# Two reorderings in a one-core two-block transformer kernel: the second long convolution's products and the second attention's value products

## The reference

```python
q_x, k_x, v_x, hy_x = jnp.split(hx @ p["w_in"], cuts, axis=-1)      # 512 tokens
v_c = heads_v(hc @ w_v)                                             # 256 context tokens
v_all = jnp.concatenate([v_c, heads_v(v_x)], axis=2)
attn_x = diff_out(diff_attn_blocked(q_x, k_all, v_all, lam), p["subln"], lam_init)
...
def hyena_mixer(proj, p, k_f):
    u = short_conv(proj, p["hy_conv_w"], p["hy_conv_b"])
    v, x1, x2 = jnp.split(u, HY_ORDER + 1, axis=-1)
    z = v
    for n, gate in enumerate((x1, x2)):
        z = gate * (long_conv(z, k_f[:, n]) + p["hy_skip"][n] * z)
    return rmsnorm(z, p["hy_norm"])
```

## Time and profile before

| | |
|---|---|
| median of three runs | 1535.79 us (1535.58 to 1537.45) |
| the profiled execution's own time | 1538.33 us |
| its span | 1536.5 us |
| PE busy | 1483.9 us, 97% of the span |
| DVE busy | 864.3 us, 56% |
| ACT busy | 621.0 us, 40% |
| POOL busy | 309.2 us, 20% |
| mean granted TensorE clock | 0.986 of full speed |

### The profile page before, as it was taken

How to read it: one execution, slowest core, us unless ns; L and a number is a source line. 1 busy time by engine, 2 the same in 40 slices (tenths; PEclk the granted TensorE clock), 3 DMA queues, 4 the chain that set the end, 5 groups by cost and what they waited for, 6 DMA issues and landing times.

```text
span 1536.5 us, 18015 instructions
## 1 busy us (share of the span) xinstructions
PE 1483.9 (97%) x7022; PEld 1209.0 (79%) x7022; DVE 864.3 (56%) x1398; ACT 621.0 (40%) x986; POOL 309.2 (20%) x296
## 2 busy tenths in 40 slices
PE   6999999999999999999998999999898999999998
PEld 5776768888878878888876878877687888888886
DVE  5455667554577564664457437777656555345434
ACT  5635773232444231334344326664335333123332
POOL 0263211101032100121004312225621111111101
PEclk9999999999999999999998999999999999999999
DMA  7352105655255344554326221223532323322321
GB/s 246 122 163 71 42 28 177 222 162 169 78 184 173 123 165 145 171 161 168 124 96 216 76 69 42 65 100 124 170 118 96 96 96 96 109 87 92 107 86 55
DMA packets 53327, 187.93 MB, mean 122 GB/s; under 512 B 5943, under 2 KB 6616, under 8 KB 53114
## 3 DMA queue, kind: packets, MB, share of 16 engines
q1 hardware_dynamic: 47450, 165.80, 32.8%
q0 software_dynamic: 4736, 16.78, 3.3%
q10 hardware_dynamic: 1056, 4.19, 0.8%
HBM read 174.16 MB, written 12.58 MB: 122 GB/s over the span
## 4 chain that ended last, share of the span: by engine, by line
PE 89%; DVE 4%; ACT 3%; issue 1%; POOL 1%; DMA 0%; SPq 0%; ACTq 0%; DVEq 0%; POOLq 0%
PE PS L458 87%; PE PS L469 2%; DVE wl L1689 1%; ACT wh L1108 1%; DVE TMP L2189 0%; ACT TMP L1201 0%; DMA X<-in_x 0%; DVE TMP L1742 0%; ACT TMP L1199 0%; POOL wl L2329 0%; DVE accm L1669 0%; DVE TMP L2152 0%; ACT TMP L1398 0%; ACT TMP L1212 0%; DVE Y L1704 0%
## 5 line engine op out<-in xcount | busy, mean ns | idle before, releaser
L1689 DVE TENSOR_TENSOR wl<-raw,wh 128x1024 fp32r<-128x1024 f32 x212 | 274.5, 1298 | 282.3 <-ACT wh L1108 281.8
L458 PE MATMUL PS<-HTh,wh 128*128 128x512 f32 x1056 | 420.8, 398 | 8.1 <-ACT TMP L1398 3.9
L458 PE MATMUL PS<-HTl,wh 128*128 128x512 f32 x1056 | 414.2, 392 | 0.0
L458 PE MATMUL PS<-HTh,wl 128*128 128x512 f32 x1056 | 413.9, 392 | 0.0
L1108 ACT ACTIVATE wh<-raw 128x1024 fp32r<-128x1024 f32 x228 | 239.0, 1053 | 280.7 <-PE PS L458 242.3
L458 PEld LDWEIGHTS PS<-HTh,wh 128*128 128x128 f32 x1056 | 200.3, 190 | 56.1 <-issue 12.4
L458 PEld LDWEIGHTS PS<-HTh,wl 128*128 128x128 f32 x1056 | 200.0, 189 | 43.2
L458 PEld LDWEIGHTS PS<-HTl,wh 128*128 128x128 f32 x1056 | 200.4, 190 | 39.0 <-issue 0.5
L458 PE MATMUL PS<-wh,FFh 128*128 128x512 f32 x432 | 169.8, 393 | 0.0
L458 PE MATMUL PS<-wh,FFl 128*128 128x512 f32 x432 | 168.8, 391 | 0.0
L458 PE MATMUL PS<-wl,FFh 128*128 128x512 f32 x432 | 168.8, 391 | 0.0
(11 more groups left out here) (322 smaller groups left out, 2134.7 us busy)
## 6 DMA issues: line engine op xcount, KB each, us to landing
raw<-in_ws SPq DMA_DIRECT2D x268, 512.0 KB, 3.8
taps<-TMP SPq DMA_DIRECT2D x16, 256.0 KB, 2.5
tab<-in_spec POOLq DMA_DIRECT2D x8, 512.0 KB, 5.8
raw<-taps SPq DMA_DIRECT2D x8, 512.0 KB, 3.9
kd<-TMP POOLq DMA_DIRECT2D x16, 256.0 KB, 6.4
wh<-in_wd POOLq DMA_DIRECT2D x8, 512.0 KB, 4.0
wl<-in_wd POOLq DMA_DIRECT2D x8, 512.0 KB, 4.7
kf<-kd SPq DMA_DIRECT2D x8, 512.0 KB, 3.7
```

Source lines behind the costliest of these rows:

```text
L458: return nc.tensor.matmul(out, l, r, start=start, stop=stop, skip_group_check=True)
L1689: tt(WL[k][:, :n], RAW[RAW_AT["unit", u, 0] % RAWS][:, :n], f32(WH[k][:, :n]), ALU.subtract).then_inc(sem("lo_dve"), 1)
```

## The change

- **Values tile by tile.** All six tiles are summed side by side for k = 0 to 5 only. The last two slices are done tile by tile, in the order `V2_TURN` = 1, 2, 3, 4, 0, 5, and `p_v2` is incremented after each. The copies wait for their own tile and go in that order.
- **Second convolution (o = 1).** TensorE issues forward 0 to 3 first, then backward 0 and 1, group 11, turn 10, backward 2 and 3, turn 11. The units of the transform matrices are packed to match (forward 0 to 3 in two units, backward 0 and 1 in one). On VectorE, ScalarE and GpSimd head 3's scaling and short convolution 10 come after spectral 5 and no longer after spectral 4.
- **Banks.** The scaling sum 3 and turn 9 take banks of `ACC`, so `RING4` serves the forward products alone. Each accumulator is asked for when its first product comes, by a fixed table `ACC_TURN`, and no longer all four at once; this holds for o = 0 too.
- **GpSimd.** `sub_low(3 * o)` comes after the low parts of f = 1, for both orders.

No product, copy or transfer is added or removed.

```diff
--- before.py
+++ after.py
@@ -100,4 +100,8 @@
         inv = [[("dft_i", t * 512 + f * P, k * P, P) for t in range(2) for k in range(2)] for f in range(4)]
-        pack(fwd[0] + fwd[1] + fwd[2] + inv[0], "pre")
-        pack(fwd[3] + inv[1], "pre")
+        if o == 0:
+            pack(fwd[0] + fwd[1] + fwd[2] + inv[0], "pre")
+            pack(fwd[3] + inv[1], "pre")
+        else:
+            pack(fwd[0] + fwd[1] + fwd[2] + fwd[3], "pre")
+            pack(inv[0] + inv[1], "pre")
         pack(colmajor("w_in_2", 1536 + (8 if o == 0 else 11) * P, 1))
@@ -397,2 +401,9 @@
 
+        V2_TURN = (1, 2, 3, 4, 0, 5)
+
+        def V2_READY(i):
+
+            return "v2_evv" if i % 2 else "v2_ev", 1 + sum(1 for j in V2_TURN[:V2_TURN.index(i)] if j % 2 == i % 2)
+
+
         EARLY_FIRST = range(2)
@@ -884,9 +895,16 @@
                     spread(3)
-            bs = [bank(("v2", i), "v2_evv" if i % 2 else "v2_ev", i // 2 + 1) for i in range(6)]
-            for k in KT:
+            bs = [bank(("v2", i), *V2_READY(i)) for i in range(6)]
+            def value_step(k, i, w):
+                h, l, o = (HCh, HCl, i) if i < 2 else (HTh, HTl, i - 2)
+                return mm3(PS[:, bs[i], :], (h[:, k, o * P:(o + 1) * P], l[:, k, o * P:(o + 1) * P]), w, k == 0, k == 7)
+
+            for k in range(6):
                 w = weights("w_in_2", k * P, D)
                 for i in range(6):
-                    h, l, o = (HCh, HCl, i) if i < 2 else (HTh, HTl, i - 2)
-                    m = mm3(PS[:, bs[i], :], (h[:, k, o * P:(o + 1) * P], l[:, k, o * P:(o + 1) * P]), w, k == 0, k == 7)
-            m.then_inc(sem("p_v2"), 1)
+                    value_step(k, i, w)
+
+            for i in V2_TURN:
+                for k in (6, 7):
+                    m = value_step(k, i, weights("w_in_2", k * P, D))
+                m.then_inc(sem("p_v2"), 1)
 
@@ -952,2 +970,4 @@
 
+            ACC_TURN = ((6, 7, 4, 5), (7, 5, 4, 6))
+
             def hyena_group(j):
@@ -959,3 +979,3 @@
             def hyena_turn(j):
-                b = bank(("ht", j), "u_ev", j + 1, RING4)
+                b = bank(("ht", j), "u_ev", j + 1, ACC if j == 9 else RING4)
                 e.wait_ge("hc_v", 6 * j + 6)
@@ -974,3 +994,3 @@
             def sub_scale(h):
-                b = bank(("sn", h), "sn_v", h + 1, RING4 if h % 2 else ACC)
+                b = bank(("sn", h), "sn_v", h + 1, RING4 if h == 1 else ACC)
                 e.wait_ge("sn_dg", 4 * h + 4)
@@ -1009,5 +1029,2 @@
                 y = n % 3
-                if f == 0:
-                    for q in range(4):
-                        bank(("acc", o, q), *(("ac_q", 2 * o + q - 1) if q > 1 else ("ac_v", 4 * o + 2 * q + 2)), ACC)
                 for c in range(2):
@@ -1015,2 +1032,6 @@
                     for q in range(2):
+                        if f == 0:
+                            a = 2 * c + q
+                            bank(("acc", o, a), *(("ac_q", 2 * o + a - 1) if a > 1 else ("ac_v", 4 * o + 2 * a + 2)),
+                                 (ACC_TURN[o][a],))
                         i = mm3(PS[:, BANK["acc", o, 2 * c + q], :], weights("dft_i", 512 * c + f * P, q * P, o),
@@ -1028,8 +1049,13 @@
                         sub_scale(1)
-                    if f in (1, 2) and o:
-                        hyena_turn(8 + f)
-                    if f >= 2:
+                    if f == 1 and o:
+                        hyena_turn(9)
+                    if f >= 2 and o == 0:
                         backward(o, f - 2)
+                if o:
+                    backward(o, 0)
+                    backward(o, 1)
 
                 hyena_group(8 + 3 * o)
+                if o:
+                    hyena_turn(10)
                 backward(o, 2)
@@ -1450,4 +1476,6 @@
                     rotated(7)
-            for i in range(0, 6, 2):
-                e.wait_ge("p_v2", 1)
+            for i in V2_TURN:
+                if i % 2:
+                    continue
+                e.wait_ge("p_v2", V2_TURN.index(i) + 1)
                 act(V2[:, i, :], PS[:, BANK["v2", i], :], ACT.Copy, scale=2.0 ** -10).then_inc(sem("v2_ev"), 1)
@@ -1556,3 +1584,3 @@
                         sub_diag(0)
-                    if f == 1 - o:
+                    if f == 1:
                         sub_high(3 * o)
@@ -2084,4 +2114,6 @@
                     rotated(7)
-            for i in range(1, 6, 2):
-                e.wait_ge("p_v2", 1)
+            for i in V2_TURN:
+                if i % 2 == 0:
+                    continue
+                e.wait_ge("p_v2", V2_TURN.index(i) + 1)
                 ts(V2[:, i, :], PS[:, BANK["v2", i], :], 2.0 ** -10, None, ALU.mult).then_inc(sem("v2_evv"), 1)
@@ -2220,5 +2252,5 @@
                         spectral(4 * o + f)
-                    if f == 1 - o:
+                    if f == 1:
                         sub_high(3 * o)
-                    if f == 0 and o:
+                    if f == 1 and o:
                         hyena_conv(10)
```

## The result

The changed kernel takes **1527.19 us** (median of 4 runs, 1526.66 to 1530.0) against 1536.62 for the kernel before (median of 4, 1535.58 to 1537.74): a ratio of 0.9948 [0.9936, 0.9959]. In a later group, with 5 runs of it and 21 of the kernel before, it is 1527.8 against 1535.36, ratio 0.9954 [0.9941, 0.9966]. So it is faster, by 7.6 to 9.4 us by the medians (7.1 to 8.0 by the ratios) where 7.9 were forecast, and the forecast time is 0.7 us off. Parts 1 and 2 gave more than it held, and the clock outside the changed code made up for the rest.

A forecast was written before the change was run, and what follows sets the result against it. TensorE, 89% of the chain that ended last, was taken as the bound, so only its waits counted. Gains of 1.7 + 0.4 + 5.8 = 7.9 us from the median 1535.79 gave 1527.9 us, range 1524.8 to 1531.8.

The forecast's parts named there:

- Part 1: Second attention's value products: closing sums one at a time removes the 1.97 us wait before first scores; 1.7 us gained.
- Part 2: First long convolution: asking for each accumulator bank separately removes backward product 0's 0.32 us wait; 0.4 us, bounds 0 and 0.5.
- the chain alone: VectorE's softmax chain behind the value copies: starts earlier by two copies of 0.63 us, moving up 1.3 us.
- The rival in which the new wait drops the clock: First softmax: a new 1.5 us wait costs a 1.4 us clock episode; total gain 6.5, time 1529.3; chance 0.15.
- Part 3: Second long convolution: reordering and lent banks bring its last turn from 1110.60 to 1104.75; 5.8 us gained.
- the locked instruction: Spectral 4's subtraction on VectorE, held up while GpSimd splits a weight unit; taken at 1.8 us.
- as the rival had it: Second convolution: VectorE bounds it, so the gain there is 4.2 us and the time 1529.5; chance 0.17.
- the port: Shared by VectorE and GpSimd: SBUF instructions exclude each other, the later blocks; as a rival, 1542.1 us, chance 0.04.
- Everything after 1111 depends on TensorE and moves with it.: Rest of the program behind the second convolution: keeps the whole 7.9 us gain.

The follow-up runs named there:

- experiment 2: Changed kernel with the value products, their one signal and the copies as before, leaving both convolutions' edits: 1530.77 us against 1535.21, ratio 0.9970.
- experiment 9: Kernel before, with only the first convolution's four accumulator banks asked for one at a time: 1533.04 us against 1535.08, ratio 0.9983.
- experiment 5: Changed kernel with VectorE doing head 3's scaling and short convolution 10 ahead of spectral 5 again: 1533.34 us against 1535.36, ratio 0.9985.
- experiment 6: Changed kernel with head 3's sum product and turn 9 back on the forward products' ring of four: 1533.94 us against 1535.36, ratio 0.9991.
- experiment 7: Changed kernel with feed-forward banks in order of the last normalisation's tiles and the first two feed-forward groups interleaved: 1526.88 us against 1535.36, ratio 0.9945.
- experiment 4: Changed kernel with feed-forward products taking banks in the order of the last normalisation's tiles: 1524.48 us against 1535.21, ratio 0.9937.
- experiment 7's second kernel: Interleaved feed-forward groups with banks in tile order, plus the second weight unit's low part made inside the last normalisation: 1523.96 us against 1535.08, ratio 0.9929.

## Why the prediction was right

**Part 1, 1.7 us forecast, 2.3 in the trace.** The events came out as written: no wait ahead of the first scores, one ahead of the second, the turn set by VectorE's chain. The new waits are 0.84 and 0.25 us instead of 1.5. The sizes match less well than the totals say. Two things were not priced. The first is the stretch at the lower clock behind the old wait, which the trace of before showed: 6.97 - 6.29 = 0.68 us by experiment 2. The sum held some 0.4 of it without naming it, as the time by which the turn came too late behind the map. Without the stretch, the distance from product to turn is 8.66 us, and 8.66 - 7.01 = 1.65 is the chain alone. The chain was forecast at 1.3, for two copies, which gave 1.2. The other 0.45 is the second thing, lambda: ScalarE is through its copies sooner, and VectorE waits 0.27 us for its exponential instead of 0.71. So 1.7 is near 1.65 by luck. The rival in which the new wait drops the clock did not happen in any of the traces with it.

**Part 2, 0.4 us forecast, 0.64 in the traces.** The mechanism is right: the wait of 0.32 went. Its price was too small, and above the bound of 0.5, since the refill behind it counts too. Nothing in the timing can show it.

**Part 3, 5.8 us forecast, 5.6 in the trace,** and 27.65 us for the stretch where 27.4 were worked out. Step by step: one wait of 0.94 at forward group 7 (0.9 forecast), no lower clock, VectorE continuous, the locked instruction where it was assumed. Of the 5.6 us, 4.1 are waits and 1.5 is the clock spell, by the execution of experiment 9 that had the waits without the spell. VectorE did not bound the stretch as the rival had it, but the wait that is left is for VectorE. Of the two instructions that the port held up, 2.88 us had slack; 1.92 us had none, and the sum rightly carried it (1.8). Experiments 5 and 6 show that both VectorE's order and the lent banks are needed: without the first, 1.1 us of the stretch's gain is left, without the second none.

**The step that failed** is the sentence "Everything after 1111 depends on TensorE and moves with it." It moved with it up to the last normalisation, 47.3 us on. There 2.1 us were lost, because lending out two banks turned the ring for every later user and put the slowest tile on the bank that the first feed-forward product needs. I had followed the lent banks to the end of the convolution and not to the end of the program. The row of ScalarE that frees this bank was in the trace of before, and the bank assignment could have been counted from the code.

**Why the number still held.** The true terms sum to 2.3 + 0.7 + 5.6 - 2.1 = 6.5 us, against 7.9. Measured were 7.6 and 9.4 by the medians, 7.1 and 8.0 by the ratios. In the two profiled executions the rest is clock spells in stretches that hold no edit, as in the table's first row; that the same makes up the 1 to 3 us between the medians is likely, since their mean granted clocks differ too, but not shown. That the total is as near as 0.7 us is luck: a missed loss, terms that were too small, and the clock outside cancelled.

## What to carry to other kernels

When an edit takes one more buffer from a ring, follow the ring to its last user: the buffers turn for everyone behind, and a place far from the edit can wait for another, later reader. Then give the first taker behind a join the buffer that is freed first; here the trace gives 3.2 us for one line against the changed kernel, of which the ring set back gives 2.6 as well. And when one execution is compared with another, take distances between landmarks around the edit, and read the granted clock beside them, before a difference of spans is put down to anything.

## What the runs showed of the hardware

The clock behind a single wait of TensorE: after the 0.94 us at forward group 7 it held in every trace. After 1.97 us it fell in the kernel before (both profiles) and held in experiments 2 and 9. After about 3.2 us it fell in three traces and held in one (experiment 9). After 2.84 (experiment 7), 3.75, 4.74 and the 3.9 to 6.0 us ahead of the feed-forward stage it fell each time. Ahead of and in the first feed-forward group, it fell behind waits of 1.25 and 0.83 us (experiment 4) and held behind 1.40 and 1.05 us (experiment 7's second kernel), so the length of one wait does not decide it. Such a spell cost 0.7 us (experiment 2), 1.5 (experiment 9), 1.7 (experiment 5) and 3.0 (experiment 6) on top of the wait, so where the clock fell, a removed wait of 3 to 5 us was worth about one and a half times its length. The Trainium skill's "TensorE: Matmul & The Clock Gate", section "A second HAM failure mode", warns of idles between groups as banks rotate; here the idles below 1 us at the forward groups did no harm, and the cost came with the few longer ones.

The 32 products of one column each (the first convolution's sums) keep TensorE busy for 3.63 us in the changed kernel's trace, and in every trace the clock was at its lower level 1.2 us behind them at the latest (in four of the 14 from the first product behind them on), though no wait of over 1.4 us stood ahead. I had priced no clock there.
